# The causal mask of an attention block, added by VectorE in PSUM or by products on TensorE

## The reference, cut to what matters

```
def forgetting_attention(q, k, v, c):
    ...
    def one_block(args):
        q_i, c_i, i = args
        s = jnp.einsum('bhqd,bhkd->bhqk', q_i, k, preferred_element_type=jnp.float32) * scale
        s = s + c_i[..., None] - c[:, :, None, :]
        qpos = i * Q_BLOCK + jnp.arange(Q_BLOCK)
        s = jnp.where(kpos[None, :] <= qpos[:, None], s, -jnp.inf)
        p = jax.nn.softmax(s, axis=-1)
        return jnp.einsum('bhqk,bhkd->bhqd', p.astype(v.dtype), v)
```

## Time and profile before

| | |
|---|---|
| median of 3 runs | 2057.54 us |
| lowest and highest of them | 2055.2 and 2060.1 us |
| the profiled execution's own time | 2055.06 us |
| its span | 2053.3 us |
| TensorE busy, of the span | 2032.8 us |
| VectorE, ScalarE, GpSimd busy | 973.5, 782.6, 855.0 us |
| attention steps a = 0 to 6, first scores to first scores | from 1498.07 to 1636.96 us |

### The profile page before, as it was taken

The page is one execution under the profiler, slowest core; times in us unless marked ns, Lnnn a source line. Parts: engine busy times, 40 slices in busy tenths (PEclk is TensorE's granted clock), DMA queues, the critical chain, the costliest instruction groups (busy, mean ns, idle before and its releaser), DMA issues.

```text
span 2053.3 us, 24438 instructions
## 1 busy us (share of the span) xinstructions
PE 2032.8 (99%) x9810; PEld 1659.2 (81%) x9810; DVE 973.5 (47%) x1481; ACT 782.6 (38%) x1123; POOL 855.0 (42%) x357
## 2 busy tenths in 40 slices
PE   9899999999999999999999999999999999999999
PEld 6788888778888888888888888888877788888887
DVE  6688888433322314534454242354356655425242
ACT  5455545634222213612332222246356643222222
POOL 3333433543444444434444444454422234444444
PEclk9999999999999999999999999999999999999999
DMA  4222222342323232323333233233321122322323
GB/s 168 81 73 83 77 88 74 113 149 91 103 92 101 94 95 90 102 93 100 96 93 103 93 93 103 93 113 93 103 63 51 53 83 93 103 93 93 103 93 113
DMA packets 55121, 194.31 MB, mean 95 GB/s; under 512 B 6112, under 2 KB 6368, under 8 KB 55008
## 3 DMA queue, kind: packets, MB, share of 16 engines
q1 hardware_dynamic: 55008, 192.75, 29.5%
HBM read 190.62 MB, written 2.10 MB: 94 GB/s over the span
## 4 chain that ended last, share of the span: by engine, by line
PE 95%; DVE 3%; ACT 1%; issue 1%; DMA 0%; POOL 0%; SPq 0%; DVEq 0%; POOLq 0%
PE ps L1285 29%; PE ps L1286 29%; PE ps L1287 29%; PE ps L1590 1%; PE ps L1623 1%; PE ps L1614 1%; PE ps L1406 1%; PE ps L1555 1%; PE ps L1554 1%; PE ps L1553 1%; PE ps L1293 1%; DVE arena L910 0%; DVE arena L749 0%; PE ps L1428 0%; DMA x<-in_xT 0%
## 5 line engine op out<-in xcount | busy, mean ns | idle before, releaser
L351 POOL TENSOR_TENSOR w_lo<-w_raw,w_hi 128x1024 fp32r<-128x1024 f32 x353 | 854.7, 2424 | 1186.3 <-ACT w_hi L368 1175.2
L1285 PE MATMUL ps<-a_hi,w_hi 128*128 128x512 f32 x1472 | 582.4, 396 | 10.1 <-DVE a_lo L767 4.8
L1287 PE MATMUL ps<-a_hi,w_lo 128*128 128x512 f32 x1472 | 574.2, 390 | 0.0
L1286 PE MATMUL ps<-a_lo,w_hi 128*128 128x512 f32 x1472 | 574.1, 390 | 0.0
L368 ACT CAST w_hi<-w_raw 128x1024 fp32r<-128x1024 f32 x353 | 366.4, 1042 | 360.2 <-PE ps L1287 323.1
L1285 PE MATMUL ps<-b_hi,w_hi 128*128 128x512 f32 x1176 | 459.3, 391 | 0.3 <-DVE x L775 0.2
L1286 PE MATMUL ps<-b_lo,w_hi 128*128 128x512 f32 x1176 | 457.6, 389 | 0.0
L1287 PE MATMUL ps<-b_hi,w_lo 128*128 128x512 f32 x1176 | 457.6, 389 | 0.0
L738 DVE TENSOR_TENSOR arena<-ps,inv_rms 128x512 f32<-128x512 f32 x200 | 138.1, 690 | 440.0 <-PE ps L1287 420.2
L1285 PEld LDWEIGHTS ps<-a_hi,w_hi 128*128 128x128 f32 x1472 | 276.8, 188 | 72.9 <-issue 11.0
L1286 PEld LDWEIGHTS ps<-a_lo,w_hi 128*128 128x128 f32 x1472 | 276.7, 188 | 58.4 <-issue 2.4
(11 more groups left out here) (192 smaller groups left out, 1586.8 us busy)
## 6 DMA issues: line engine op xcount, KB each, us to landing
w_raw<-in_panels SPq DMA_DIRECT2D x353, 512.0 KB, 3.5
x<-in_xT SPq DMA_DIRECT2D x16, 256.0 KB, 3.0
outT<-x SPq DMA_DIRECT2D x8, 256.0 KB, 2.6
consts<-in_const SPq DMA_DIRECT2D x1, 528.5 KB, 7.8
arena<-in_rows SPq DMA_DIRECT2D x1, 256.0 KB, 4.6
arena<-in_ws SPq DMA_DIRECT2D x1, 256.0 KB, 4.7
consts<-in_late SPq DMA_DIRECT2D x1, 168.0 KB, 2.6
params<-in_param SPq DMA_DIRECT2D x1, 116.0 KB, 2.1
```

The source lines that it names most:

```text
L351: nc.gpsimd.tensor_tensor(w_lo[:, p % RING, :], w_raw[:, p % RING, :], w_hi[:, p % RING, :].bitcast(F), ALU.subtract).then_inc(w_low, 1)
L1285: nc.tensor.matmul(o, wh, hi[:, kt, :], start=(kt == 0), stop=False)
L1286: nc.tensor.matmul(o, wh, lo[:, kt, :], start=False, stop=False)
L1287: ins = nc.tensor.matmul(o, wl, hi[:, kt, :], start=False, stop=(kt == tiles - 1))
```

## The change

The mask leaves TensorE's list, and each forgetting product (L1595) becomes the last of its group and counts up `scored`. VectorE adds a 128 x 128 array `mask` (0 and -1e30, float) from SBUF to the diagonal block in PSUM before the reduction of b = 3, 2 and 1; the add ahead of b = 2 spans two blocks, its own diagonal block and the block b = 0 beside it in the bank. Each add is a `link`: VectorE waits for it. The counts and the order of the reductions stay. The constants `mask_q` and `mask_k` (192 columns of 336) give way to `mask` (128 of 272), which come with one load in an earlier part.

```
-for _name, _n in [("halves", P), ("mask_q", 3 * P // 4), ("mask_k", 3 * P // 4), ("onehot", HEADS_A)]:
+for _name, _n in [("halves", P), ("mask", P), ("onehot", HEADS_A)]:
...
                     dve.wait_ge(scored, a * 2 * BLK + before)
+
+                    if b > 0:
+                        blocks = 2 if b == 2 else 1
+                        got = ps[:, bk, at + b * P:at + (b + blocks) * P].rearrange("p (j n) -> p j n", j=blocks)
+                        link(v.tensor_tensor(got, got, c("mask").unsqueeze(1).broadcast_to([P, blocks, P]), ALU.add))
                     v.tensor_reduce(row_neg[:, side * BLK + b:side * BLK + b + 1], ps[:, bk, at:at + P * (b + 1)],
                                     AX.X, ALU.max, negate=True).then_inc(maxed, 1)
...
-                                         forget[half_of(side), 0:P * (b + 1)], start=False, stop=False)
-                    for n in range(2):
-                        part = slice((1 - n) * HEAD_DIM, (1 - n) * HEAD_DIM + P)
-                        for side in range(2):
-                            bk, at = SCORES[side, b]
-                            ins = nc.tensor.matmul(ps[:, bk, at + b * P:at + (b + 1) * P], mask_q[half_of(side), part],
-                                                   mask_k[half_of(side), part], start=False, stop=(n == 1))
-                            if n == 1:
-                                ins.then_inc(scored, 1)
+                                         forget[half_of(side), 0:P * (b + 1)], start=False, stop=True).then_inc(scored, 1)
...
-            "mask_q": bf16(band == 0), "mask_k": bf16(np.where(band > 0, NEG, 0.0)),
+            "mask": np.where(t[None, :] > t[:, None], NEG, 0.0),
```

More of the change, by code:

```diff
@@ L1577, in _ @@
                 values(m)
-            mask_q, mask_k = c("mask_q").bitcast(BF), c("mask_k").bitcast(BF)
             pe.wait_ge(k_normed, DT)
@@ L1676, in packed @@
         return np.ascontiguousarray(a.reshape(P, -1)).view(np.float32)
-    def bf16(a):
-        return packed((np.ascontiguousarray(a, np.float32).view(np.uint32) >> 16).astype(np.uint16))
-    band = np.arange(3 * HEAD_DIM)[None, :] - HEAD_DIM - t[:, None] % HEAD_DIM
     parts = {"ident": np.eye(P), "ones": np.ones((P, P)), "eps": np.full((P, 1), EPS), "reset": reset,
```

## The result

The changed kernel is slower: median 2065.84 us of 11 runs (2063.31 to 2082.04) against 2058.64 us of 11 runs (2055.12 to 2060.27) of the kernel before, ratio 1.0051 with a 95% interval of 1.0036 to 1.0066. The ratio weighs all runs and stands for some 10.5 us; the two medians lie 7.2 us apart, because a few runs of the changed kernel are much longer than its median. 5.8 us were forecast. The median lies inside the stated range and the sign is the forecast one, but the forecast size is little more than half of what the ratio gives. Two things in these numbers are not in the forecast at all: the changed kernel's runs spread over 19 us, and the execution whose trace the forecast rests on (2055.06 us) is one of the fastest of the kernel before, not a typical one.

The account below looks back on a forecast made before the run. TensorE's list plus its few waits was taken as the bound. Costs of 1.41 us (a = 0), 3.2 (six steps) and 1.25 (a = 7), saving included, gave 5.8 us: 2063.4 us on the median, range 2055 to 2068 us.

Parts of the forecast that it names:

- What bounds the kernel: TensorE, busy 2032.8 of 2053.3 us; mid-step it waits for VectorE's low_sq, set by a chain over four engines.
- Taken from TensorE: Removing 128 mask products saves 0.48 us a step, 3.8 us over 8 steps; at most 4.7 us.
- Given to VectorE: Four adds of 0.32 us and two of 0.45 us a step, each waited for: 2.18 us a step.
- first rival: Waits on VectorE's adds cost nothing, adds take 0.19 and 0.33 us: 1.4 us in all, 2058.9 us; chance 0.20.
- Steps 1 to 6, undisturbed: Exponentials 0.70 us late, GpSimd holds the scalings, TensorE waits 1.0 us: each step 0.53 us longer, 3.2 us for six.
- Step a = 0: First attention step: exponentials and GpSimd 1.42 us late, square_sums start 1.41 us later, counted as the step's cost.
- Step a = 7: Last attention step: later low_hid and scalings hold out3 and the second set of transposes; 1.25 us later.
- The sum: Over the attention steps, 1.41 + 3.2 + 1.25 = 5.8 us slower, TensorE's saving already included.
- third rival: GpSimd's second subtraction starts before low_sq, which waits 2.4 us, seven times: some 16 us more, about 2079 us; chance 0.06.
- The base: Forecast set against the profiled execution, 2055.06 us, giving 2060.9; on the median of runs, 2057.54 us, giving 2063.4.

Follow-up runs that it names:

- e2: Changed kernel with both panels' high parts moved later in ScalarE's list, so neither GpSimd subtraction starts before VectorE's side 1 scalings and low_sq are done: 2052.20 us, ratio 0.9962.
- e3: Changed kernel without VectorE's adds, so neither engine applies the mask: 2055.71 us, ratio 0.9982.
- e1: Changed kernel with the second panel's high part moved behind the probability copies in ScalarE's list, so GpSimd's second subtraction asks later: 2062.34 us, ratio 1.0014.
- e5: Kernel before with the second panel's high part moved behind the copies in ScalarE's list, first subtraction left in place: 2055.25 us, ratio 0.9984.
- e8: Kernel before, unchanged, traced a second time: 2059.11 us.
- e4: Kernel before with VectorE's adds put in as well, so the mask is applied twice: 2080.84 us, ratio 1.0103.

## Why the prediction was right or wrong, point by point

**What bounds the kernel.** Right: TensorE's list plus waits, and in the steps 0 to 6 the one wait that matters is square_sums on low_sq. What it leaves out is the clock at which the list runs behind a wait.

**Taken from TensorE.** Too small: 0.61 us a step (e2, e3), where 0.48 was taken and 0.59 was the upper end. The choice to leave half of the last group's distance in place was right: a block of query rows takes 0.13 us less where 0.12 was taken, for the first and the last one. The two blocks between gave back 0.18 us each. The error is that one group, at 0.12 us, was taken for all four. Scores of the four blocks and the next product in the changed kernel's step a = 1; the starts lie 1.20, 0.82, 0.28 and 0.70 us apart, where before (1518.64, 1519.96, 1520.97, 1521.43, 1522.27) they lay 1.33, 1.00, 0.47 and 0.83 us apart, which sums to 0.63 us:

```profile
1525.15 1.13 PE L1593 MATMUL ps<-arena 64*128 64x512 f32 x4
...
1526.35 0.81 PE L1593 MATMUL ps<-arena 64*128 64x384 f32 x4
...
1527.17 0.39 PE L1593 MATMUL ps<-arena 64*128 64x128 f32 x4
...
1527.45 0.65 PE L1593 MATMUL ps<-arena 64*128 64x256 f32 x4
...
1528.15 0.50 PE L1290 MATMUL ps<-a_hi,w_hi 128*128 128x512 f32 x1
```

**Given to VectorE.** Right: the adds took 291 and 427 ns on average, and the next instruction started 0.03 us behind their end, so 0.32 and 0.46 us against 0.32 and 0.45. The first rival (waits that cost nothing) is out. The Trainium skill (VectorE: DVE Perf Modes, section on the TRN2 errata) gives (N + 151) / 0.96 ns for a float tensor_tensor add and has compared it at 512 and 2048 columns. Estimates by that formula are 291 ns at 128 columns and 424 ns at 256, and the measured means of 291 and 427 ns agree.

**Steps 1 to 6, undisturbed.** Right in every link. Exponential 0.68 us later (0.70), GpSimd 0.67 (0.70), scalings held until 1.07 us after its end (1.07), square_sums 13.20 us into the step (13.24), the undisturbed step 20.19 us (20.25). By the distance of starts TensorE waited 1.1 us (square_sums 13.20 us into the step, 12.11 in e2 without a wait) where 1.0 was forecast; the row shows 0.83, counted from the end of the transposes, which is modelled.

**Step a = 0.** The position of square_sums was right, 1.45 us later in e1 (1.41). The wait was not: "about 2.0 us" leaves out that TensorE comes earlier by what it saved, 0.6 us, and e1 shows 2.67. Failed: "later by 1.41" was taken for the cost of the step. Behind the wait of 2.67 us TensorE's clock is at its lower level, and the step costs 3.06. No sentence of the prediction priced what a wait does to the clock.

**Step a = 7.** Right, a little high: 1.06 us where 1.25 was forecast, with three waits of 0.35, 0.43 and 0.30 us on low_hid and the two sets of scalings.

**The sum.** For undisturbed steps 5.8 us was forecast; e1 against e5, both with the second subtraction away, differ by 7.1 us in their medians (on two chips), and the steps' differences between e1 and the first trace of before give 3.06 + 2.8 + 1.06 = 6.9. The missing part is the clock at a = 0, 1.6 us, against 0.6 us of the other terms' errors the other way.

**The third rival is where the size went wrong: the step that failed.** The sum put GpSimd's second subtraction at nothing, since GpSimd "stood back until both were done". The runs showed 9.1 of the 16.0 us of the profiled execution, and 3.5 us of the median, in its place (the changed kernel against e1). The rival that held this had a chance of 0.06 and a price of 2.4 us "seven times", as one thing that happens in all steps or in none. It is neither: it happened in three of seven steps in one execution, with 2.1 to 2.2 us of wait and up to 1.7 us of slow clock each on top of e1's step. That its number differs between executions was traced for the kernel before alone (e8); for the changed kernel it is inferred from the spread of 2063 to 2082 us, which e1 brings down to 3.4 us but for one run. The evidence against it was one row, GpSimd's subtraction of 3.23 us at a = 0. That row showed one outcome of a meeting that can go either way, and e8 shows the same meeting, at the same distance of 0.32 us, with the other outcome. The rule of the Trainium skill (SBUF — State Buffer, section on the two separate sides), that whoever starts first holds the ports for its whole instruction, agrees with these traces: low_sq at 2.82 us spans the rest of a subtraction. The prediction set it aside for one row.

**Why the meeting takes place.** At a = 1 the second subtraction used to ask at 1531.08, when low_sq, 0.68 us from 1530.34, was done; nothing met. With the first subtraction lying fully on the scalings, low_sq starts 0.30 to 0.32 us behind the second one's request in each of the steps 1 to 6. Without that delay the scalings, 1.28 us from 1534.97, would end at 1536.25 and low_sq would be done before the request at 1537.20. So the first collision makes the second one. This is worked out from the rows; no run moved the first subtraction alone.

**The base.** The forecast was set against an execution of 2055.06 us. The kernel before meets GpSimd at a = 0 anyway and loses there in most executions: 21 of 23 runs beside e1 to e4 and 12 of 21 beside e5 to e8 are in its slower group, whose step a = 0 e8 shows. The changed kernel's a = 0 loses 6.2 us against the lucky trace and 2.4 against the usual one. That the median of 2065.84 us lies in the stated range is luck in part: the upper end of the range was there for dearer adds, and the adds cost what was forecast.

## What to carry to other kernels

Before an engine in the middle of a chain is given work, ask which work of its neighbours was placed to miss it, and move that first: here the same adds cost some 10 us, or came with a gain of 2 us, by the place of two lines in ScalarE's list. Where a row shows that two engines met and one stood back, take it for one throw, and price the other outcome for each such meeting; a second trace, or two groups in the kernel's own run times, tells it. Price a wait of about 3 us on TensorE with the products behind it at half clock: 1.6 to 1.7 us on top of the wait in e1, e8 and the changed kernel's a = 6, and nothing in its a = 3.

## What the runs showed of the hardware

A request of GpSimd that comes 0.30 to 0.32 us before VectorE's low_sq, while VectorE is busy with the scaling ahead, went either way: it stood back in steps 1, 2, 4 and 5 of the changed kernel and in the first trace of before, and went first in the steps 3 and 6 and in e8. In e4 it went first in the steps 1 to 5, at 0.32 to 0.34 us, and stood back in step 6, at 0.31. The distance in the trace doesn't sort the cases; what decides stays open. At a = 0 of the changed kernel, of e3 and of e4 the request comes within the scalings, at 1511.69, 1509.86 and 1510.92 us, and it went first all three times.

TensorE's granted clock fell to 0.50 with waits of 2.67 (e1), 2.77 (e8), 2.89 and 2.90 (five times in e4), 2.97, 3.31 (e3), 4.19 (e4) and 4.75 us, never with waits of 0.8 us; with the wait of 2.98 us at a = 3 of the changed kernel it stayed at 1.00 (step 22.33 us, against 23.98 at a = 6 with 2.97 us). The low level lasted longer behind the waits of 4.75 us and of a = 3 in e4: from square_sums to the next scores these steps took 9.65 and 9.83 us, against 8.6 us in e1 and e8 and 7.0 us at full clock. A wait of that length brings it or not by something that the traces don't show.
